# Expert weight rows ordered so that on-chip tiles hold neighbouring columns, the last w_up run loaded in two chunks, and one instead of two pairs of tiles gathered transposed

## What is computed

```
p = rms_norm(x) @ w_in;  three branches (attention, short conv, memory attention), gated, @ w_out
x1 = x + merged @ w_out
h2 = rms_norm(x1)
logits = h2 @ w_router + b_router;  top 4 of 32 experts, softmax over the four
for e in range(32):
    glu, lin = split(h2 @ w_up[e] + b_up[e])          # w_up[e]: 1024 x 2048
    a = min(glu, 7) * sigmoid(1.702 * min(glu, 7)) * (clip(lin, -7, 7) + 1)
    y = y + combine[:, e] * (a @ w_down[e] + b_down[e])   # w_down[e]: 1024 x 1024
out = x1 + y
```

## Time and profile before

| | |
|---|---|
| median of three runs | 1185.5 us (1183.97 to 1186.59) |
| profiled execution | 1183.96 us, its span 1181.8 us |
| TensorE busy | 1138.4 us, 96% of the span |
| VectorE / ScalarE / GpSimd busy | 385.3 / 276.3 / 79.0 us |
| moved by DMA | 449.62 MB, mean 380 GB/s |
| mean granted TensorE clock | 0.987 of full speed |

### The profile page before, as it was taken

One profiled execution on the slowest core, in us unless ns is written; L12 is line 12 of the kernel. 1 busy time (PEld: TensorE's weight loads), 2 busy tenths in 40 slices (PEclk: granted clock), 3 DMA queues, 4 the chain that ended last, 5 costly groups with the idle time before them and its releaser, 6 DMA issues.

```text
span 1181.8 us, 13597 instructions
## 1 busy us (share of the span) xinstructions
PE 1138.4 (96%) x5611; PEld 541.7 (46%) x5611; DVE 385.3 (33%) x707; ACT 276.3 (23%) x430; POOL 79.0 (7%) x99
## 2 busy tenths in 40 slices
PE   8999999999999999999999999999999999999987
PEld 7879988885333333333333333333333333333332
DVE  5767865553222222222222312222221212122212
ACT  6765364442111112111111111111111101011001
POOL 6424340000000000000000000000000000000000
PEclk9999999999999999999999999999999999999998
DMA  7454449986999999999999999999999999999995
GB/s 263 168 221 150 158 160 379 376 351 262 426 437 427 429 434 433 429 430 435 430 427 436 431 428 432 434 428 431 434 429 433 433 430 429 431 435 427 431 428 233
DMA packets 25123, 449.62 MB, mean 380 GB/s; under 512 B 3378, under 2 KB 3506, under 8 KB 6148
## 3 DMA queue, kind: packets, MB, share of 16 engines
q1 hardware_dynamic: 23472, 447.23, 89.7%
q10 hardware_dynamic: 1620, 1.95, 0.5%
HBM read 448.12 MB, written 1.05 MB: 380 GB/s over the span
## 4 chain that ended last, share of the span: by engine, by line
PE 69%; DMA 25%; DVE 3%; issue 1%; ACT 0%; another core or an unknown queue 0%; POOL 0%; DVEq 0%; SPq 0%; POOLq 0%; ACTq 0%
PE aux L1765 28%; DMA ring<-w_up_dram 25%; PE acc L1569 14%; PE aux L1843 12%; PE acc L1562 3%; PE aux L1664 3%; PE acc L1748 2%; PE aux L1674 1%; PE aux L1795 1%; DVE w_lo L956 1%; PE aux L1822 1%; DVE pick_w L1225 1%; DMA raw<-w_front_dram 1%; PE aux L1828 1%
## 5 line engine op out<-in xcount | busy, mean ns | idle before, releaser
L1765 PE MATMUL aux<-ring,xgT 128*64 128x512 f32 x2048 | 464.9, 604 | 23.9 <-DMA ring<-w_up_dram 22.6
L1765 PEld LDWEIGHTS aux<-ring,xgT 128*64 128x64 f32 x2048 | 147.5, 139 | 313.9 <-issue 265.3
L1843 PE MATMUL aux<-ring,aT 128*64 128x512 f32 x992 | 225.0, 595 | 0.0
L1305 DVE TENSOR_SCALAR glu<-aux 128x512 f32<-128x512 f32 x32 | 22.1, 692 | 372.7 <-PE aux L1765 372.7
L956 DVE TENSOR_TENSOR w_lo<-raw,w_hi 128x1024 fp32r<-128x1024 f32 x80 | 103.6, 1316 | 50.8 <-ACT w_hi L715 50.8
L1843 PEld LDWEIGHTS aux<-ring,aT 128*64 128x64 f32 x992 | 66.6, 136 | 112.4 <-issue 107.3
L897 ACT ACTIVATE sig<-glu 128x512 f32<-128x512 f32 x32 | 20.2, 632 | 393.2 <-DVE glu L1305 393.2
L715 ACT ACTIVATE w_hi<-raw 128x1024 fp32r<-128x1024 f32 x80 | 84.1, 1061 | 88.2 <-PE acc L1569 62.8
L906 ACT ACTIVATE y_hi<-aux,slot_w 128x512 fp32r<-128x512 f32 x31 | 21.4, 690 | 246.7 <-PE aux L1843 246.7
L1569 PE MATMUL acc<-w_hi,hT_hi 128*128 128x512 f32 x188 | 76.1, 405 | 1.5 <-DVE hT_lo L968 1.5
L1569 PE MATMUL acc<-w_lo,hT_hi 128*128 128x512 f32 x188 | 73.9, 393 | 0.0
(11 more groups left out here) (326 smaller groups left out, 1052.2 us busy)
## 6 DMA issues: line engine op xcount, KB each, us to landing
ring<-w_up_dram SPq DMA_DIRECT2D x56, 4096.0 KB, 47.8
ring<-w_down_dram SPq DMA_DIRECT2D x26, 4096.0 KB, 45.3
raw<-w_front_dram SPq DMA_DIRECT2D x39, 1024.0 KB, 5.0
ring<-w_up_dram SPq DMA_DIRECT2D x15, 2048.0 KB, 11.2
ring<-w_down_dram SPq DMA_DIRECT2D x10, 2048.0 KB, 11.2
ring<-w_down_dram SPq DMA_DIRECT2D x8, 512.0 KB, 45.6
ring<-w_up_dram SPq DMA_DIRECT2D x2, 1024.0 KB, 4.8
x<-x_dram SPq DMA_DIRECT2D x2, 512.0 KB, 4.1
```

Source lines behind the costliest of these rows:

```text
L1305: nc.vector.tensor_scalar(glu[:], bank_glu[:], LIMIT, None, ALU.min).then_inc(glu_ready, 1)
L1765: ins = nc.tensor.matmul(bank[64 * half:64 * half + 64, :], xgT[:, k], w_rows[:, c0 + half * W:c0 + (half + 1) * W], start=(k == 0), stop= ...
L1843: ins = nc.tensor.matmul(bank[64 * half:64 * half + 64, :], turned[:, j, 64 * ff_half:64 * ff_half + 64], w_rows[:, half * W:(half + 1) * ...
```

## The change

On the host, w_up and w_down of each expert are stored with their rows permuted (`up_runs`, `down_runs`), so that the same loads bring rows 128j+p of the block to tile j on partition p. Tiles then match 128 neighbouring columns of tokens and activation; all transposes and gathers read neighbouring columns, b_up and the columns of w_up keep their order, and the second copy of the scale goes. The last w_up run (chunks 2 and 3 of expert 32) becomes two loads of 2 MB. In the first item one pair (k=0, 1) is gathered transposed; tiles 2 and 3 are gathered with tokens in rows in `gather_rest`, 128 more columns for each half, copied by ScalarE with the others, transposed as one more 128x128 block and moved by VectorE ahead of tiles 4 to 7. The bias products move from after k=2 to after k=1.

```diff
--- before.py
+++ after.py
@@ -42,8 +42,7 @@
 
 C_G1, C_GM, C_G2, C_CONV = 0, 8, 16, 24
 C_XQ, C_XK, C_FQ, C_FK, C_BF = 36, 37, 38, 39, 40
-C_G2_UP = 41
-NCOLS = 49
+NCOLS = 41
 
 
 R_NEG, R_POS, R_END = 64, 96, 104
@@ -309,7 +308,6 @@
         acc = [ctx.enter_context(nc.psum_tensor(f"acc{b}", [P, W], F32)) for b in range(4)]
         aux = [ctx.enter_context(nc.psum_tensor(f"aux{b}", [P, W], F32)) for b in range(4)]
         bank_glu, bank_lin, bank_cy, bank_t = aux
-        pair_bank = [bank_cy, bank_t]
 
 
         x_loaded = [sem(f"x_loaded{t}") for t in range(NT)]
@@ -426,10 +424,11 @@
             return sum(1 for g in range(end) if g % RING == slot and signals_use(g % CHUNKS))
 
         last_downs = [g for g in range((NEXP - 2) * CHUNKS, NEXP * CHUNKS) if g % CHUNKS >= UP_CHUNKS]
+        last_up_run = [(NEXP - 1) * CHUNKS + UP_CHUNKS - 2, (NEXP - 1) * CHUNKS + UP_CHUNKS - 1]
 
         def in_run(g):
 
-            return g >= FIRST_RUN and g not in last_downs
+            return g >= FIRST_RUN and g not in last_downs + last_up_run
 
         def begins_run(g):
 
@@ -885,7 +884,7 @@
                 nc.scalar.activation(soft[:, t], logits[:, t], ACT.Exp, bias=ntop[:, t:t + 1]).then_inc(soft_ready, 1)
 
             act.wait_ge(tok_gathered, 1)
-            nc.scalar.activation(xg_tok[:, 0:2 * P], acc[2][:, 0:2 * P], ACT.Copy).then_inc(tok_copied, 1)
+            nc.scalar.activation(xg_tok[:, 0:3 * P], acc[2][:, 0:3 * P], ACT.Copy).then_inc(tok_copied, 1)
 
             def copy_gathered(n):
                 act.wait_ge(gathered, n - 1)
@@ -1233,24 +1232,23 @@
             def move_gathered(n):
                 dve.wait_ge(xg_turned, n - 1)
                 order = "p (h q) -> p q h"
-                gain = cols[:, C_G2_UP:C_G2_UP + KD].rearrange(order, h=2).unsqueeze(3)
+                gain = cols[:, C_G2:C_G2 + KD].rearrange(order, h=2).unsqueeze(3)
                 nc.vector.tensor_tensor(xgT[:].rearrange("p (h q) s -> p q h s", h=2),
                                         bank_glu[:].rearrange("p (q h s) -> p q h s", q=KD // 2, h=2),
                                         gain.to_broadcast([P, KD // 2, 2, SLOTS]), ALU.mult).then_inc(xg_ready, 1)
 
-            def move_pair(pair):
-                dve.wait_ge(pair_gathered, pair + 1)
+            def move_pair(pair, bank):
                 k = slice(2 * pair, 2 * pair + 2)
-                gain = cols[:, C_G2_UP + 2 * pair:C_G2_UP + 2 * pair + 2].unsqueeze(2)
-                nc.vector.tensor_tensor(xgT[:, k], pair_bank[pair][:, 0:2 * SLOTS].rearrange("p (k s) -> p k s", k=2),
+                gain = cols[:, C_G2 + 2 * pair:C_G2 + 2 * pair + 2].unsqueeze(2)
+                nc.vector.tensor_tensor(xgT[:, k], bank.rearrange("p (k s) -> p k s", k=2),
                                         gain.to_broadcast([P, 2, SLOTS]), ALU.mult).then_inc(pair_ready, 1)
 
             build_bias_sel(slice(0, 1))
             dve.wait_ge(slots_ready, 2)
             nc.vector.tensor_copy(count[:, 0:1], bank_glu[0:96, 0:1]).then_inc(extra_ready, 1)
             nc.vector.tensor_tensor(pos_tab[:, :, 0:NEXP], slots, chosen, ALU.mult).then_inc(table_ready, 1)
-            move_pair(0)
-            move_pair(1)
+            dve.wait_ge(pair_gathered, 1)
+            move_pair(0, bank_cy[:, 0:2 * SLOTS])
 
             dve.wait_ge(soft_ready, 2)
             chained(nc.vector.tensor_tensor(soft[:], soft[:], chosen, ALU.mult))
@@ -1260,7 +1258,8 @@
                                     top_den[:, :, 1:2].to_broadcast([P, NT, NEXP]), ALU.mult).then_inc(table_ready, 1)
 
             dve.wait_ge(tok_turned, 1)
-            gain = cols[:, C_G2_UP + 4:C_G2_UP + 8].rearrange("p (h j) -> p j h", h=2).unsqueeze(3)
+            move_pair(1, acc[1][:, 2 * P:3 * P])
+            gain = cols[:, C_G2 + 4:C_G2 + 8].rearrange("p (h j) -> p j h", h=2).unsqueeze(3)
             nc.vector.tensor_tensor(xgT[:, 4:8].rearrange("p (h j) s -> p j h s", h=2),
                                     acc[1][:, 0:2 * P].rearrange("p (j h s) -> p j h s", j=2, h=2),
                                     gain.to_broadcast([P, 2, 2, SLOTS]), ALU.mult).then_inc(pair_ready, 1)
@@ -1670,19 +1669,17 @@
 
                 pe.wait_ge(xg_tok_ready, n - 1)
                 for q in range(UP_RUN):
-                    rows = xg_tok[:].rearrange("s (p j) -> s j p", j=UP_RUN)[:, q]
-                    ins = nc.tensor.transpose(bank_glu[:, q * P:(q + 1) * P], rows, ident[:])
+                    cs = slice(q * P, (q + 1) * P)
+                    ins = nc.tensor.transpose(bank_glu[:, cs], xg_tok[:, cs], ident[:])
                 ins.then_inc(xg_turned, 1)
 
-            def gather_pair(pair):
-
-                bank = pair_bank[pair]
+            def gather_pair():
+
                 for t in range(NT):
-                    if pair == 0:
-                        pe.wait_ge(pick_ready, t + 1)
+                    pe.wait_ge(pick_ready, t + 1)
                     for i in range(2):
-                        rows = x1[:, t, 0:W].rearrange("s (p j) -> s j p", j=UP_RUN)[:, 2 * pair + i]
-                        ins = nc.tensor.matmul(bank[:, i * SLOTS:(i + 1) * SLOTS], rows, pick[:, t],
+                        rows = x1[:, t, i * P:(i + 1) * P]
+                        ins = nc.tensor.matmul(bank_cy[:, i * SLOTS:(i + 1) * SLOTS], rows, pick[:, t],
                                                start=(t == 0 and i == 0), stop=(t == NT - 1), skip_group_check=True)
                 ins.then_inc(pair_gathered, 1)
 
@@ -1690,21 +1687,24 @@
 
                 for t in range(NT):
                     for half in range(2):
-                        cs = x1[:, t, W:D].rearrange("s (p h j) -> s h p j", h=2, j=UP_ROWS)[:, half]
+                        cs = x1[:, t, (UP_ROWS + half) * P:(UP_ROWS + half + 1) * P]
+                        nc.tensor.matmul(acc[2][64 * half:64 * half + 64, 2 * P:3 * P], pick[:, t], cs,
+                                         start=(t == 0), stop=False, skip_group_check=True)
+                        cs = x1[:, t, W + 2 * half * P:W + 2 * (half + 1) * P]
                         ins = nc.tensor.matmul(acc[2][64 * half:64 * half + 64, 0:2 * P], pick[:, t], cs,
-                                               start=(t == 0), stop=(t == NT - 1), skip_group_check=True)
+                                               start=False, stop=(t == NT - 1), skip_group_check=True)
                 ins.then_inc(tok_gathered, 1)
 
             def turn_rest():
                 pe.wait_ge(tok_copied, 1)
+                nc.tensor.transpose(acc[1][:, 2 * P:3 * P], xg_tok[:, 2 * P:3 * P], ident[:])
                 for j in range(UP_ROWS):
-                    rows = xg_tok[:, 0:UP_ROWS * P].rearrange("s (p j) -> s j p", j=UP_ROWS)[:, j]
-                    ins = nc.tensor.transpose(acc[1][:, j * P:(j + 1) * P], rows, ident[:])
+                    cs = slice(j * P, (j + 1) * P)
+                    ins = nc.tensor.transpose(acc[1][:, cs], xg_tok[:, cs], ident[:])
                 ins.then_inc(tok_turned, 1)
 
             keep_up(KEEP_UP[2])
-            for pair in range(2):
-                gather_pair(pair)
+            gather_pair()
             pe.wait_ge(extra_ready, 1)
 
 
@@ -1788,7 +1788,7 @@
                         gather_rest()
                     if first_item and k == 1:
                         turn_rest()
-                    if k == (2 if first_item else 0):
+                    if k == (1 if first_item else 0):
                         pe.wait_ge(bias_sel_ready, n)
                         for bank, c0 in ((bank_glu, 0), (bank_lin, FF)):
                             for half in range(2):
@@ -1812,8 +1812,8 @@
             def turn_activation(n):
                 pe.wait_ge(a_ready, n)
                 for j in range(DOWN_ROWS):
-                    ins = nc.tensor.transpose(bank_t[:, j * P:(j + 1) * P],
-                                              sig[:].rearrange("s (p j) -> s j p", j=DOWN_ROWS)[:, j], ident[:])
+                    cs = slice(j * P, (j + 1) * P)
+                    ins = nc.tensor.transpose(bank_t[:, cs], sig[:, cs], ident[:])
                 ins.then_inc(aT_done, 1)
 
             def turn_weights(n):
@@ -1949,11 +1949,13 @@
     cols[:FOX_D, C_FQ], cols[:FOX_D, C_FK] = a["fox_q_g"][0], a["fox_k_g"][0]
     spread = np.ascontiguousarray(np.broadcast_to(a["b_router"][0][None, :], (P, NEXP)))
 
-    cols[:, C_G2_UP:C_G2_UP + KD] = a["norm2_g"][0].reshape(KD // UP_RUN, P, UP_RUN).transpose(1, 0, 2).reshape(P, KD)
-
-    def by_down_run(w):
-        parts = w.reshape(*w.shape[:-1], 2, P, 2, DOWN_ROWS)
-        return np.ascontiguousarray(parts.swapaxes(-3, -2)).reshape(w.shape)
+    def up_runs(w):
+        rows = w.reshape(NEXP, KD // UP_RUN, UP_RUN, P, 2 * FF).swapaxes(2, 3)
+        return np.ascontiguousarray(rows).reshape(w.shape)
+
+    def down_runs(w):
+        rows = w.reshape(NEXP, DOWN_RUN, P, D).swapaxes(1, 2)
+        return np.ascontiguousarray(rows).reshape(w.shape)
 
```

(4 more changed lines are left out.)

## The result

The changed kernel took 1180.66 us in the median of six runs (1178.62 to 1182.25) beside 1186.13 us for the kernel before (1183.97 to 1187.24): ratio 0.9955, 95% interval 0.9942 to 0.9967. Two repetitions later gave 0.9965 (0.9954 to 0.9976) and 0.9958 (0.9945 to 0.9971). So the gain is 4.1 to 5.3 us by the ratios and 3.0 to 5.5 by the medians; 3.7 us, that is 1181.8, had been forecast. The profiled execution took 1181.00 us, span 1178.8.

A forecast was written before the change was run, and what follows sets the result against it. The stream of expert weights was taken to bound the kernel; 3.05 us at the restart, 0.37 from the split and 0.3 from transposes gave 3.7 us, 1181.8 us from a median of 1185.5, range 1180.0 to 1184.2.

The forecast's parts named there:

- What bounds it: Whole kernel: the stream of expert weights sets the pace; its restart, at the end of k=3, comes 3.05 us earlier.
- The gather: First item: one pair gathered from neighbouring columns takes 1.3 us, weight loads near 190 ns; k=0 starts 2.3 us earlier.
- rival (b): Gather and transposes: strides cost nothing, 64-column products set the old rate; total gain 2.6 us, 1182.9; chance 0.05.
- (e): Restart: stationary reads stay slow for another reason and k=2 waits 0.8 us instead of 0.1; 1183.6 us; chance 0.06.
- The clock: Restart, k=0: the clock stays at full speed because dense products begin before the old fall; 1.4 us gained.
- My own sign of being wrong: Among the signs listed as wrong: a granted clock of 0.5 between 280 and 290 us, at the restart.
- Rival (a): Restart: the clock falls as before; 1.6 us gained there instead of 3.05, total 2.3 us, 1183.2; chance 0.22.
- The rest of the gather: First item, before k=1: eight more 128-column records at 0.08 us each cost 0.65 us (0.4 to 1.1).
- The new wait: First item, before k=2: waiting for pair 1 from VectorE, mostly filled by bias products, costs 0.1 us (0 to 0.4).
- The last items: Experts 31 and 32: splitting the last w_up run removes a 0.37 us wait; contiguous transposes save 0.3 us.
- Rival (c): Restart: a later release, item 1's first w_down chunk, holds the stream; 0.5 us lost, 1182.3; inside the forecast's 0.62.
- (d): Stream's rate: row placement or the cut run makes it 0.73% slower, 6.3 us; about 1188 us; chance 0.05.

The follow-up runs named there:

- the cut runs: Changed kernel, second w_up runs of experts 30 and 31 also cut in two: 1179.38 us; plus expert 31's second w_down chunk by rows: 1178.41 us.
- two pairs: Changed kernel with both pairs of the first item gathered transposed again, from neighbouring columns: medians 1180.74 us (ratio 0.9956) and 1180.16 us (0.9959).
- the idle products: Changed kernel with two idle 512-column products between the gather of the pair and k=0: median 1181.67 us, ratio 0.9967.

## Why the prediction was right, and where not

**What bounds it: right in the main.** The stream has the same rate in all profiles to 1 GB/s, and what is gained before the issue of slot 1 is gained at the end, give or take what the stream itself varies (below). With A as the measure, the kernel before has 14.22, 15.19 and 15.50 us (its two profiles and that of the split alone), mean 14.97; the changed restart has 12.87, 12.88, 11.19 and 11.19, mean 12.03. That is 2.9 us, where 3.05 was forecast.

**The gather: right.** 1.12 us forecast as 1.3; the start of k=0 is 1.58 us after it (1.7 forecast). The weight load is 192 ns, the 190 that the one row of another line had shown. With the step alone put back it is 330 ns and the gather 2.14 us, so the price of the step is shown, and rival (b), and with it (e), falls. The rule of the Trainium skill on SBUF's 16-byte lines ("SBUF — State Buffer", Specifications) agrees with 330 against 192 ns; its rule for LDWEIGHTS ("TensorE: Matmul & The Clock Gate"), by which only the columns count, doesn't.

**The clock: wrong as stated, the size right by luck.** I took one state for the whole and said that the clock stays up. My own sign of being wrong, a clock of 0.5 between 280 and 290 us, is there in two of the three profiles of the changed kernel. The clock fell at the restart in four of four profiles with the step (the three of the old form and the step put back) and in two of ten without it (both of the changed kernel; four others with the same restart stayed up, two of them with the cut runs, A = 11.20). So with the step it fell more often; what makes it fall isn't shown, and the profiles are few. Rival (a) is thus a share of the executions rather than another outcome, and it costs 1.69 us there (12.88 - 11.19). Its own figure, 1.6 us gained, was 0.3 too high, since 1.55 us of gather don't fit into 2.56 us at half speed; the first two profiles give 1.35.

What I had mis-sized on the other side is what the old kernel pays: 1.3 us by the first profile, 2.2 and 2.6 by the two others, 2.0 in the mean. Taken off, A is 12.94 or 12.95 us in all three. So of the 2.9 us of A, 1.75 are the shorter chain (12.94 - 11.19, forecast 3.05 - 1.4 = 1.65) and 1.2 are the clock: 2.0 us lost before and 0.85 after, where I had 1.4 and nothing. The two errors nearly cancel, which is why the mean of A came out right; that is luck.

**The rest of the gather: right,** 1.32 to 1.34 us where 1.55 was forecast; the rows 0.24 and 0.22 for four 128-column records each give 0.06 a record (0.08). **The new wait: right,** bias and wait 0.55 (0.43 + 0.1).

**One pair instead of two** was worked out only together with the order of columns. Taken apart, it is -0.3 us: what it saves at the start it pays in the rest of the gather. Eight records less save 0.88 us of gather (2.00 - 1.12), VectorE's move, no longer hidden, takes back 0.47, and the rest, the third transpose and the wait take more than what is left. The terms all stood in my sum, but I didn't set them against each other.

**The last items: a small miss.** The wait that the split removes was one execution's: there it cost 0.6 us, in the other two it wasn't there, and the split brought nothing in the time. The transposes brought 0.18 us of C (46.31 - 46.13, both with the split) where 0.3 was forecast, and not as divided: the group of L1815 went from 0.68 to 0.59 us, not by 0.24. I had taken the spacing of 0.11 us from a group of two; four are 0.15 apart. The larger thing there I named only as a danger: a fall of the clock after the wait for expert 31, 1.7 us, is in six of the eight profiles with the new order that keep that run whole, and in none of the three of the old form.

**The surplus.** The profiles can be added up. The old form (before twice, the split alone) took 1185.8 us in the mean, the new one (the changed kernel three times, once without the split) 1181.55: 4.3 us less. Of these A has 2.9, the start of the gather 0.2 and what follows C 0.2. C itself is worse by 0.9 (46.53 against 47.41), because the clock fell in three of the four. The remaining 1.8 us lie in B: 835.7, 837.9 and 838.0 us in the old form, 836.1, 834.9, 835.0 and 835.4 in the new. This I had not forecast. But B is 837.3 and 836.4 with two pairs and 835.4 with the step put back, which share the new order of rows, and in the first comparison it is 0.4 us longer after the change. So it follows neither the rows' order nor the form of the gather cleanly; whether the 1.8 us are more than a draw stays open.

**Rival (c) is where a part of B's spread arises.** The load that waits for the first w_down chunk of item 1 is issued 14.73 us after slot 1 in the old order and 14.55 after it in the new: the transposes of the first item do count, by 0.18 us, and I had put all but the last items at nothing. By the prediction's estimate DMA has about then worked off what it had. In the ten microseconds from 15 to 25 us after the issue of slot 1 the core moved 424, 411 and 393 GB/s in the old form (in the order of B above), 419 and 405 with two pairs, and 423 to 433 in the changed kernel, without the split, with the step put back and with the idle products. The lowest, that of the split alone, and for comparison the first one of the changed kernel:

```profile
309.36:319.36 10.00, 10.00 (x52) 3.49 (x50) 0.99 (x2) 2.17 (x3) 0.00 (x0) 1.00 0.99 393
```

```profile
305.77:315.77 10.00, 10.00 (x50) 3.40 (x48) 0.99 (x2) 2.17 (x3) 0.00 (x0) 1.00 1.01 423
```

The four profiles at 419 or below are the four with the longest B, 836.4 us and more. At 432 GB/s the lowest, 393, is 0.9 us of traffic missing, an estimate. So the stream can lose up to that here, more than the 0.5 us of (c), in both forms. Why it loses it in one execution and not in another isn't shown, and the rest of the spread isn't placed.

That the forecast of 3.7 us came close to the measured 4.1 to 5.3 thus rests on the shorter chain at the restart, which was right, on two errors about the clock there that cancel, and on C and B, of which one was lost and the other came unforeseen.

Two small sums of the prediction are off and change nothing: the worked times end at 289.6, not 289.5 (286.05 + 1.87 + 1.72), and in (d) 6.3 us against a gain of 3.7 would be a loss of 2.6, not 2.4.

## What to carry to other kernels

Where a stream of loads sets the pace, look for the few us in which it stands still, and price every record of the chain that restarts it; in the middle TensorE waits for DMA, and what it saves there only lengthens the wait. At the restart, and where TensorE works off its last loads, cut the loads that are waited for as wholes, but look at which wait comes last: the cut of the last run alone brought nothing, the cuts before it and of the chunk behind it 3 us, a part of which may be a clock that no longer fell. Take several profiles of each kernel before pricing such a stretch. A stationary f32 operand read with a step of four costs 1.7 times its weight load (330 against 192 ns); ordering weights on the host takes that away for nothing.

## What the runs showed that I had not expected

A profile is one draw of the clock. The changed kernel fell to 1.2 GHz at the restart in one execution and not in the next. The old one was down there in both of its profiles, but back at full clock at 284.95 us in one and at 287.2 in the other. Later the clock falls at the 2.1 us wait of an item (8.78 us for 32 records instead of 7.09), though not at each: rows 11 have such a wait with 7.09 behind it. In the middle of the stream this is free, since the next wait gets shorter by it (0.82 instead of 2.1 us); at the restart and behind the last wait it is 1.7 us each, and the spread of the changed kernel's runs, 3.6 us in the first comparison, is of that size.
